# Six output tiles of a normalised projection computed from the unnormalised stream, with the token factor and the projected shift applied afterwards

## What is computed

```
mod = silu(c) @ w_ada + b_ada                 # nine vectors of 1024: sh1, sc1, gt1, sh2, sc2, gt2, ...
u = rmsnorm(h, g1) * (1 + sc1) + sh1
h = h + 0.5 * gt1 * swiglu(u, w_ffn1)         # "w1"
u = rmsnorm(h, gm) * (1 + sc2) + sh2          # site "nm"
h = h + gt2 * token_mixing(u, ...)            # proj = u @ w_in: pool (256), q, k, v (768 each), gates (2048)
u = rmsnorm(h, g2) * (1 + sc3) + sh3          # site "n2"
h = h + 0.5 * gt3 * swiglu(u, w_ffn2)         # "w2"

rmsnorm(x, g) = x * rsqrt(mean(x * x over the features) + 1e-6) * g
```

## Time and profile before

| | |
|---|---|
| runs | 2529.46, 2530.55, 2534.22 us; median 2530.55 |
| the profiled execution | 2532.03 us, of which its span 2530.2 us |
| TensorE matmul busy | 2445.1 us (97%), 15654 matmuls |
| VectorE busy | 1801.1 us (71%) |
| ScalarE busy | 1106.5 us (44%) |
| DMA | 454.72 MB, mean 180 GB/s |
| granted TensorE clock | 0.99 of full, mean |

### The profile page before, as it was taken

One profiled execution on the slowest core, in us unless ns is written; L12 is line 12 of the kernel. 1 busy time (PEld: TensorE's weight loads), 2 busy tenths in 40 slices (PEclk: granted clock), 3 DMA queues, 4 the chain that ended last, 5 costly groups with the idle time before them and its releaser, 6 DMA issues.

```text
span 2530.2 us, 39280 instructions
## 1 busy us (share of the span) xinstructions
PE 2445.1 (97%) x15654; PEld 2226.9 (88%) x15654; DVE 1801.1 (71%) x3467; ACT 1106.5 (44%) x1656; POOL 0.2 (0%) x4
## 2 busy tenths in 40 slices
PE   4998999999999999999999999999999999998998
PEld 3998989999999888788888998888998888988997
DVE  7888887788977446768877669897785344676555
ACT  3444565544463324724223662232562222566443
POOL 0000000000000000000000000000000000000000
PEclk8999999999999999999999999999999999999999
DMA  8997656769855431653543256676374333122653
GB/s 317 334 332 266 211 193 191 250 234 313 304 196 188 140 100 59 208 159 125 154 141 121 85 183 202 192 237 199 119 241 148 94 125 95 62 92 91 202 185 99
DMA packets 161671, 454.72 MB, mean 180 GB/s; under 512 B 17745, under 2 KB 21329, under 8 KB 161489
## 3 DMA queue, kind: packets, MB, share of 16 engines
q1 hardware_dynamic: 161488, 452.21, 54.3%
HBM read 451.09 MB, written 1.05 MB: 179 GB/s over the span
## 4 chain that ended last, share of the span: by engine, by line
PE 77%; DVE 4%; ACT 4%; issue 1%; DMA 0%; ACTq 0%; DVEq 0%; SPq 0%
PE PS L1297 24%; PE PS L1299 24%; PE PS L1298 24%; DVE own L1803 1%; PE PS L1457 1%; PE PS L1324 1%; PE PS L1322 1%; ACT own L1525 1%; ACT Uh L1588 1%; PE PS L1506 1%; ACT NT L1592 1%; DVE X L1784 1%; PE PS L1489 0%; DVE X L1899 0%; ACT spare L1525 0%
## 5 line engine op out<-in xcount | busy, mean ns | idle before, releaser
L1297 PE MATMUL PS<-Uh,own 128*128 128x256 f32 (+1 forms) x2080 | 655.1, 315 | 30.4 <-DVE Ul L1888 21.7
L1298 PE MATMUL PS<-Ul,own 128*128 128x256 f32 (+1 forms) x2080 | 646.6, 311 | 0.0
L1299 PE MATMUL PS<-Uh,own 128*128 128x256 f32 (+1 forms) x2080 | 646.4, 311 | 0.0
L1525 ACT ACTIVATE own<-raw 128x1024 fp32r<-128x1024 f32 x425 | 443.3, 1054 | 360.9 <-PE PS L1299 298.6
L1803 DVE TENSOR_TENSOR own<-raw,own 128x1024 fp32r<-128x1024 f32 x425 | 515.0, 1220 | 76.6 <-ACT own L1525 76.2
L1297 PEld LDWEIGHTS PS<-Uh,own 128*128 128x128 f32 x2080 | 401.5, 193 | 55.4 <-issue 29.5
L1298 PEld LDWEIGHTS PS<-Ul,own 128*128 128x128 f32 x2080 | 401.8, 193 | 19.8 <-issue 0.2
L1299 PEld LDWEIGHTS PS<-Uh,own 128*128 128x128 f32 x2080 | 401.6, 193 | 19.7
L1297 PE MATMUL PS<-Hh,own 128*128 128x256 f32 (+1 forms) x1088 | 345.2, 317 | 0.0
L1298 PE MATMUL PS<-Hl,own 128*128 128x256 f32 (+1 forms) x1088 | 340.9, 313 | 0.0
L1299 PE MATMUL PS<-Hh,own 128*128 128x256 f32 (+1 forms) x1088 | 340.9, 313 | 0.0
(11 more groups left out here) (233 smaller groups left out, 3866.6 us busy)
## 6 DMA issues: line engine op xcount, KB each, us to landing
MODS<-in_mm SPq DMA_DIRECT2D x168, 256.0 KB, 3.8
SCR<-in_mm SPq DMA_DIRECT2D x136, 256.0 KB, 4.3
raw<-in_f0i SPq DMA_DIRECT2D x68, 512.0 KB, 4.2
raw<-in_f1i SPq DMA_DIRECT2D x56, 512.0 KB, 3.6
raw<-in_f2i SPq DMA_DIRECT2D x56, 512.0 KB, 3.6
SCR<-in_ma SPq DMA_DIRECT2D x88, 256.0 KB, 5.3
raw<-in_w1i SPq DMA_DIRECT2D x44, 512.0 KB, 5.4
raw<-in_w2i SPq DMA_DIRECT2D x44, 512.0 KB, 5.4
```

The lines of the kernel that those rows point to most:

```text
L1297: e.matmul(o, ll, rh, start=start, stop=False, skip_group_check=shared)
L1298: e.matmul(o, lh, rl, start=False, stop=False, skip_group_check=shared)
L1299: return e.matmul(o, lh, rh, start=False, stop=stop, skip_group_check=shared)
L1525: e.activation(parts(w.n)[0], raw[:, w.n % RING, :], ACT.Copy).then_inc(s["whi"].tell(w.n), 1)
```

## The change

The first six output tiles (two pool, four q) no longer multiply u. They multiply the raw stream times the feature coefficient, g * (1 + sc2), which is ready before the norm's factor is; the shift is two more columns of the same operand. The tile that comes out holds W(x * c) in columns 0 to 255 and W * shift in column 256; eviction multiplies the first with the token's factor and adds the second. The norm still makes u for all later tiles. The raw parts lie in the context half of Uh and Ul, which is free then; the two tensors grow from 512 to 514 columns.

```diff
+RAW = 6
 def kept_tile(self, st, c, slab, at, qs, mm, banks, first, final, norm, raw):
+            self.raw_lows()
             for k in (mm,) if alone else (mm - 1, mm):
                 self.square(self.tallies[LAT], k)
+                if raw:
+                    self.put("rawhi", st=raw, k=k, after=(st, at, k, 0))
+                    self.raws.append((raw, k))
+    def raw_lows(self):
+        for site, k in self.raws:
+            self.put("rawlo", st=site, k=k)
+        self.raws.clear()
+    def raw_tile(self, name, i, first, last, n=None, bank=None):
+        if n is None:
+            n, bank = self.chunk(name, i), self.bank()
+        w = self.put("rawmm", st=name, n=n, bank=bank, k=first, f=last)
+        if last == KT:
+            self.used[n] = (w.id, 0)
+        return w
 def schedule(total):
-    p.rate = 1.5
-    main = p.ffn("w1", "w1o", LAT, [(("w1", 0), "half", 0, 2)], False)
+    p.rate = 1.7
+    def before_raw():
+        p.column(("nm", "c"), "gm", 0, 4)
+        p.mod_until(0, 3)
+        p.put("rawshift", q=0, f=3)
+        p.rate = 0.0
+    main = p.ffn("w1", "w1o", LAT, [...], False, then={len(SLABS) - 1: before_raw}, raw="nm")
-    p.rate = 0.9
-    first = p.rms("nm", 0, 3, "gm", (0, 0), w1_last, 0, ("wpqk", [("wpqk", t_) for t_ in range(3)]))
     p.put("padding")
-    for t_ in range(2):
-        p.of_feature("pool_in", first, t_, "wpqk", k=t_)
-    for step in range(4):
-        p.put("pool_sum", k=step)
+    p.norming = True
+    t = p.tallies.pop(LAT)
+    raw = [p.raw_tile("wpqk", 0, 0, 6)]
+    p.raw_lows()
+    while t["todo"]:
+        p.sums(t)
+    raw[0] = p.raw_tile("wpqk", 0, 6, KT, raw[0].n, raw[0].bank)
+    p.put("stat", n=t["n"], r=LAT, bank=t["bank"], eps=1e-6)
+    raw.append(p.raw_tile("wpqk", 1, 0, KT))
+    p.put("root", n=t["n"], r=LAT)
+    p.release(t)
+    def raise_one():
+        i = raw.index(None)
+        w, raw[i] = made[i], 0
+        what, k = ("pool_in", i) if i < 2 else ("qk1", i - 2)
+        p.put(what, st="wpqk", n=t["n"], k=k, j=i, bank=w.bank, after=(w.id, 0), raw=True)
+    made, raw = raw, [None] * RAW
+    for k in range(0, KT, 2):
+        for kk in (k, k + 1):
+            p.put("rms", st="nm", k=kk, ...)
+        if len(made) < RAW:
+            made.append(p.raw_tile("wpqk", len(made), 0, KT))
+        raise_one()
+    p.put("rms", st="nm", k=KT, ...)
+    p.norming = False
+    while None in raw:
+        raise_one()
+    p.rate = 0.6
-    for t_ in range(12):
+    for t_ in range(RAW - 2, 12):      # pool_sum after the first of these; the rotations of the
...                                     # four raw q tiles follow one per tile, the rest in the values' stage
+    p.rate = 0.9                       # values, as before
-    p.rate = 0.6
+    p.rate = 0.75                      # scores
-    p.rate = 0.9
+    p.rate = 1.2                       # gates
-    p.rate, p.mod_limit = 1.4, EARLY_PAIRED * 16
+    p.rate, p.mod_limit = 1.6, EARLY_PAIRED * 16        # w2
# TensorE
+                elif w.what == "rawmm":
+                    for k in range(w.k, w.f):
+                        on.wait_ge(s["raw_lo"], k)
+                        m = three(PS[:, w.bank[0], 0:S + 2], *weights(w.n, k), Uh[:, k, S:2 * S + 2],
+                                  Ul[:, k, S:2 * S + 2], k == 0, k == KT - 1)
# ScalarE
+                elif w.what == "rawhi":
+                    e.activation(Uh[:, w.k, S:2 * S], X[:, w.k, 0:S], ACT.Copy, scale=cf((w.st, "c"))[:, w.k:w.k + 1])
+                elif w.what in ("pool_in", "qk1") and w.raw:
+                    on.wait_ge(s["raised"], w.j)
+                    e.activation(dst, dst, ACT.Identity, bias=lift[:, w.j:w.j + 1])
# VectorE
+                elif w.what == "rawlo":
+                    on.wait_ge(s["raw_hi"], w.k)
+                    e.scalar_tensor_tensor(out=Ul[:, w.k, S:2 * S], in0=X[:, w.k, 0:S], scalar=cf(...)[:, w.k:w.k + 1],
+                                           in1=Uh[:, w.k, S:2 * S].bitcast(F32), op0=ALU.mult, op1=ALU.subtract)
+                elif w.what in ("pool_in", "qk1") and w.raw:
+                    e.tensor_copy(lift[:, w.j:w.j + 1], PS[:, b, S:S + 1])
+                    e.tensor_tensor(dst, PS[:, b, 0:S], RS[:, 0, 0, :], ALU.mult)
```

More of the change, by code:

```diff
@@ L138 @@
     kept: bool = False
+    raw: bool = False
 class Plan:
@@ L549, in hidden_by_now, with kept_tile @@
                 f()
-    def kept_tile(self, st, c, slab, at, qs, mm, banks, first, final, norm):
+    def kept_tile(self, st, c, slab, at, qs, mm, banks, first, final, norm, raw):
         per = 8 // len(slab)
@@ L578, in out_tile, with outer @@
         return w
-    def outer(self, st, w_out, first, slab, at, qs, r, norm=None, banks=None, final=False):
+    def outer(self, st, w_out, first, slab, at, qs, r, norm=None, banks=None, final=False, raw=None):
         per = 8 // len(slab)
@@ L586, in outer @@
             if banks:
-                w = self.kept_tile(st, c, slab, at, qs, mm, banks, first == 0, final, norm)
+                w = self.kept_tile(st, c, slab, at, qs, mm, banks, first == 0, final, norm, final and raw)
             else:
@@ L618, in ffn @@
     def ffn(self, st, w_out, r, gates, norm, slabs=SLABS, base=0, width=FS, early=0, alone=0, at=0,
-            then={}, ahead=(), further=0):
+            then={}, ahead=(), further=0, raw=None):
         firsts = [sum(len(x) for x in slabs[:n]) for n in range(len(slabs))]
@@ L631, in out @@
             return self.outer(st, w_out, firsts[n], slabs[n], n + at, [slots[f] for f in slabs[n]],
-                              LAT if n < alone else r, norm, banks, n == len(slabs) - 1)
+                              LAT if n < alone else r, norm, banks, n == len(slabs) - 1, raw)
         for n, slab in enumerate(slabs):
@@ L705, in schedule @@
         p.put("cond", q=who, n=who)
-    p.rate = 1.5
-    main = p.ffn("w1", "w1o", LAT, [(("w1", 0), "half", 0, 2)], False)
+    p.rate = 1.7
[4 more added lines that the diff above has]
+        p.rate = 0.0
+    main = p.ffn("w1", "w1o", LAT, [(("w1", 0), "half", 0, 2)], False, then={len(SLABS) - 1: before_raw}, raw="nm")
     p.put("ctxload")
@@ L733, in context_hidden @@
         yield
[L735 to L736 removed]
     p.put("padding")
[L738 to L742 removed]
+    p.norming = True
[17 more added lines that the diff above has]
+        for kk in (k, k + 1):
+            p.put("rms", st="nm", k=kk, n=t["n"], r=LAT, after=w1_last, q=0, f=3)
+        if len(made) < RAW:
+            made.append(p.raw_tile("wpqk", len(made), 0, KT))
+        raise_one()
+    p.put("rms", st="nm", k=KT, n=t["n"], r=LAT, after=w1_last, q=0, f=3)
+    p.norming = False
+    while None in raw:
+        raise_one()
+    p.rate = 0.6
+    pending, pooling = list(range(RAW - 2)), [0, 1, 2, 3]
     def rope_one():
@@ L746, in rope_one @@
         p.put("rope1", k=i, bank=p.bank())
-    for t_ in range(12):
-        if t_:
-            p.project("wpqk", 2 + t_, "wpqk", "qk1", LAT, k=t_)
-        else:
-            p.of_feature("qk1", first, 2, "wpqk", k=t_)
-        if pending:
+    for t_ in range(RAW - 2, 12):
+        p.project("wpqk", 2 + t_, "wpqk", "qk1", LAT, k=t_)
+        pending.append(t_)
+        if t_ == RAW - 2:
+            for step in range(4):
+                p.put("pool_sum", k=step)
+        else:
             rope_one()
[L755 to L759, removed]
+            if pooling:
+                p.put("pool_mean", k=pooling.pop(0))
+    p.rate = 0.9
     for blk in range(3):
@@ L1221, in build @@
         last_mix = (find("mix", f=CT - 1).id, 0)
+        last_raw = (max(w.id for w in plan.order if w.what == "rawmm"), 0)
         last_score1, last_gather1 = (find("score1", k=7).id, 2), (find("gather1", k=7).id, 0)
@@ L1335, in tensor @@
                             m.then_inc(s["matmul"].tell(("feature", n, w.r)), 1)
+                elif w.what == "rawmm":
+                    on.wait_ge(s["wlo"], w.n)
+                    if w.k == 0:
+                        claim(w.bank)
+                    for k in range(w.k, w.f):
+                        on.wait_ge(s["raw_lo"], k)
+                        m = three(PS[:, w.bank[0], 0:S + 2], *weights(w.n, k), Uh[:, k, S:2 * S + 2], Ul[:, k, S:2 * S + 2],
+                                  k == 0, k == KT - 1)
+                    if w.f == KT:
+                        m.then_inc(s["matmul"].tell((w.id, 0)), 1)
                 elif w.what in ("gate", "up", "pool_in", "qk1", "qk2") and w.after:
@@ L1575, in scalar @@
                         on.wait_ge(s["modded"], mod_key(2, 0))
+                        on.wait_ge(s["matmul"], last_raw)
                     elif w.what == "fin":
```

45 lines of the change are left out of this document (40 added, 5 removed).

## The result

| | before | changed |
|---|---|---|
| median | 2531.51 us | 2549.30 us |
| runs | 4, 2529.46 to 2534.22 | 4, 2547.34 to 2551.16 |
| profiled execution / its span | 2532.03 / 2530.2 us | 2551.16 / 2549.3 us |

The changed kernel takes 1.0070 times as long (95% interval 1.0055 to 1.0085), 17.8 us more. Forecast were 2522.3 us and a gain.

The account below looks back on a forecast made before the run. TensorE bounds the kernel, so time is saved only where it stands or runs at low clock. Seam -10.2 and n2 +2.0 give -8.2 us: 2530.55 - 8.2 = 2522.3 us, range 2517.5 to 2528.5.

Parts of the forecast that it names:

- The seam: From w1's end through six output tiles: raw tiles don't wait for the norm, done at 261.7 us, gain 10.2 us.
- every matmul on u in the whole kernel reads them: Slower rival's ground: over 8,500 matmuls read Uh and Ul, whose rows grow to 2056 bytes; decides from 1.6 ns each.
- a rival at 0.06: Whole kernel, wider Uh and Ul slow matmuls on u: 2535.7 us and more, seam's gain gone; chance 0.06.
- n2: Site n2: the coefficient comes at about 508.9 instead of 502.5 us, delaying TensorE; +2.0 us, between 0 and 4.5.
- Six forced steps: At n2, 170 modulation steps done where 176 are needed, so six issue at once on VectorE; part of +2.0 us.
- That holds: VectorE after 270 us: 0.6 modulation steps a chunk instead of 0.9 make room for four moved rotations, about 1.1 us each.
- 0, at most +1: In w2, modulation rate 1.4 to 1.6 takes VectorE from 0.92 to about 0.99 busy: 0, at most +1 us.
- w1 at 1.7: In w1, 1.7 modulation steps a chunk add 18 GB/s of DMA: 0 us taken, +1.6 if 334 GB/s were the ceiling.
- full share would be 352: DMA in w1: a share of 0.95 for 334 GB/s makes full share 352 GB/s, just 334 + 18.

Follow-up runs that it names:

- wider rows alone: Kernel before with only Uh and Ul widened from 512 to 514 columns, the added columns never written or read: 2545.3 us against 2532.9, ratio 1.0052.
- without its layout: Whole change, but Uh and Ul keep 512 columns and all addresses stay; raw stream and shift columns lie over hidden slots 0 to 3: 2533.2 us, ratio 1.0008.
- rows of 2080 bytes: Changed kernel with Uh and Ul 520 columns wide instead of 514, so Hh and what follows lie 512 bytes on: 2544.1 us, ratio 1.0045.

## Why the prediction was wrong

**The seam: right.** Forecast were a stop of 4.1 us, six tiles done 24.2 us after w1's end, one spell of 3.4 us at low clock and a gain of 10.2. The changed kernel has 3.9, 24.3, one spell of 3.4 us, and 9.8 us of gain against the kernel with wider rows alone (10.7 against the kernel before). The stop for line 1888 and the one for a `low` after the fourth tile are gone. First sum at 239.28 instead of 241.75: w1's last matmul started 2.4 us earlier.

**The step that failed: "every matmul on u in the whole kernel reads them".** The sum has no term for the wider tensors. They were a rival at 0.06, on the ground that no row had another stride; where the trace has no row, I took the cost as nothing and put the doubt into a chance. That the threshold named for it (1.6 ns for each of 8,500, 13.3 us) lies near the 12.4 us measured is luck: it was the size from which the rival would decide, and no estimate of it. Its reach was wrong: not only matmuls on Uh and Ul are hit but Hh and Hl too, through their addresses, and 512-column ones alone pay (about 4,100 by 5 ns, 20 us) while some 8,800 of 256 columns give back 1 ns each. The wider rows cost 12.4 us by themselves and 16.1 in the changed kernel. This step alone doesn't make the miss: without its layout the change takes 2533.2 us where 2522.3 were forecast. The other 10.9 us are the work's order, at n2, in the scores and at f0, as told below.

**The test that would have missed it.** I would have been "wrong if a 256-column matmul on Uh is no longer 0.12 us from the next". That one went to 119 ns. The loss sits in the 512-column form, for which the prediction named no row and no test.

**n2: mechanism right, size off threefold.** Six forced steps: +2.0 forecast, 0 to 4.5 as bounds, 6.2 measured. VectorE at n2 in the changed kernel:

```profile
496.52 0.08 DVE L1907 DVE_READ_ACCUMULATOR2_ANT M<- 128x1 f32 x1
500.45 0.75 DVE L1907 CUSTOM_DVE_ANT_0 SCR<-SCR,M 128x512 f32<-128x512 f32 x1 [3.86 <-DMA SCR<-in_ma]
...
501.92 0.17 DVE L1928 SCALAR_TENSOR_TENSOR CF<-M,V 128x8 f32<-128x8 f32 x1
502.01 2.83 DVE L1868 SCALAR_TENSOR_TENSOR X<-PS,CF,X 128x256 f32<-128x256 f32 x7
```

Four steps at once, then 3.9 us for the fetch of the last two, the coefficient, and seven adds that had queued up: just the order that was forecast. The stop is 4.2 us instead of the 2.3 forecast, and the sum left out the low clock behind it. The first line is behind the score's stop, the second behind this one:

```profile
338.10:344.90 6.80, 6.78 (x25) 0.51 0.37 125
502.50:509.30 6.80, 6.76 (x34) 0.55 0.20 73
```

6.8 us at a granted clock of 0.5 (1.2 GHz) after the score's stop and after this one, 3.4 us of full clock lost. For the seam I had counted such a spell; at n2 I hadn't, and so the upper bound was too low as well.

**The scores: "That holds" failed.** Fewer steps were to make up for the moved rotations. Counts of VectorE's busy time can't show what decided: not how much work, but a step or two of 0.75 us in the wrong place, ahead of the adds that free the score's banks. 5.7 us were lost (2.3 us of stop where 0.7 were, and low clock). At the start of f0, where the prediction had no term beyond w2's "0, at most +1", 2.9 were lost: a stop of 1.7 us and a spell behind it. w2's rate wasn't the cause; with one step fewer at n2, and so another order, that stop is 0.4 us.

**w1 at 1.7: right.** No wait of TensorE from 60 to 190 us, 1096 matmuls, 346 GB/s at a DMA share of 0.97. The 334 GB/s of the earlier trace rows were no ceiling. The Trainium skill ("DMA: Bandwidth & Descriptors", Bandwidth) gives about 358 GB/s for the HBM side of a core. As a ceiling the traces don't bear it out: from 20 to 40 us the kernel before moves 395 GB/s and the changed one 409, and the latter 369 from 620 to 640 us; here the measurement decides. Nor is the "full share would be 352" of the prediction a ceiling, worked out from a share of 0.95: the share reads 1.04 in the first of these stretches.

**Sum by measured terms**, in the profiles: wider rows +12.8, w1 -0.4, seam -9.8, scores +5.7, n2 +6.2, f0 +2.9, later +1.7: +19.1, the difference of the two spans. Forecast were -8.2: the wider rows make 12.8 of the 27.3 missed, and 14.5 are the scores, n2 (above its +2.0), f0 and later.

## What to carry to other kernels

A change of a tensor's width or place changes the distance of every pair of operands behind it. Price it for the whole program, by shape, and test it alone, since it costs one line; if a tensor must grow, look for room elsewhere first, as with the hidden slots here. Filler that a planner spreads by a running credit moves as a whole when one rate changes: compare the two orders around the tight places, item by item, not the counts. And count a stretch at low clock as a likely part of a stop's price, not a fixed one: at the seam and at n2 each stop of 2 us and more came with 3.4 to 10.2 us of it, the score's stop with 3.4 or 6.8 at 1.2 to 2.4 us and with none at 0.7 or 0.8. But near 1850 us a stop of 2.0 to 2.3 us, in every kernel here, was followed by 3.4 us in some profiles (changed, wider rows alone) and by none in others (before, rows of 2080 bytes).

## What the runs showed of the hardware

The pace of back-to-back float32r matmuls depends on the distance between the weights' address and the moving tensor's, modulo 256 bytes. At 0: 227 ns for 512 columns, 120 for 256. At the four others tried, 32, 64, 96 and 128 bytes: 229 to 234 and 117 to 119, in the median of a pair. That the period is 256 bytes rests on distances of 256 and 512. These are paces at full clock, without waits, from matmuls between 60 and 2300 us. Why one width gains where the other loses stays open, and so does why one of three products at 64 bytes is spared. The Trainium skill ("TensorE: Matmul & The Clock Gate", Wait — 56ns, not 53.3ns?) puts the distance of back-to-back matmuls at N / 2.4 GHz + about 2.5 ns, 215.7 ns for 512 columns; for 256 the formula gives 109.2, an estimate. In the median no pair here came closer than 227 and 117, each with its own weight load, and the rule has no term for addresses; here the measurement decides.
